# Grouped attention and convolution in one block of a two-block network: order of exponential and copy, of maxima, of keys' factors, of v's products and of the convolution's steps

## What is computed

```python
# even layer, h = rms_norm(x, norm_even): 512 x 1024
a_x, a_b, a_c, a_z, b_u, b_z = split(h @ w_in)            # six parts of 512 columns
conv = sum(pad(a_c * a_x)[:, tap:tap + s] * conv_w[tap] for tap in range(3))
y_a = a_b * conv * silu(a_z)
y_b = real(fft2(b_u)) * silu(b_z)
x = x + concatenate([y_a, y_b]) @ w_out
# odd layer, h = rms_norm(x, norm_odd): 8 heads of queries, 2 of keys and values, width 128
q, k, v, z = split(h @ w_in)
q, k = apply_rope(rms_norm(q, q_gain)), apply_rope(rms_norm(k, k_gain))
p = softmax(q @ k.T * 128 ** -0.5)                        # 512 x 512 for each of 8 heads
x = x + (concatenate(p @ v) * silu(z)) @ w_out
out = rms_norm(x, final_norm)
```

## Time and profile before

| what | us |
|---|---|
| median of 3 runs | 2379.01 |
| the profiled execution itself | 2379.91 |
| its span in the profile | 2378.1 |
| PE busy | 2148.1 (90%) |
| DVE busy | 1263.6 (53%) |
| POOL busy | 1059.9 (45%) |
| ACT busy | 825.9 (35%) |

### The profile page before, as it was taken

The page is one execution under the profiler, slowest core; times in us unless marked ns, Lnnn a source line. Parts: engine busy times, 40 slices in busy tenths (PEclk is TensorE's granted clock), DMA queues, the critical chain, the costliest instruction groups (busy, mean ns, idle before and its releaser), DMA issues.

```text
span 2378.1 us, 57690 instructions
## 1 busy us (share of the span) xinstructions
PE 2148.1 (90%) x23340; PEld 1810.4 (76%) x23340; DVE 1263.6 (53%) x1988; ACT 825.9 (35%) x2166; POOL 1059.9 (45%) x651
## 2 busy tenths in 40 slices
PE   6799999988999999985979989999897989898877
PEld 4598889978888888885979947777696866676555
DVE  6756566564665666666257414454315292457454
ACT  1644444444655555553021123333202001111431
POOL 1133343323333233327857802222585877775135
PEclk8899999999999999996989999999898999998999
DMA  2234433455344334413212211101022321221002
GB/s 92 90 128 157 151 147 147 168 161 113 69 90 92 72 68 92 92 43 119 95 58 85 89 45 36 35 18 36 27 88 97 109 73 43 66 93 54 18 1 71
DMA packets 158977, 197.86 MB, mean 83 GB/s; under 512 B 121040, under 2 KB 123344, under 8 KB 156496
## 3 DMA queue, kind: packets, MB, share of 16 engines
q1 hardware_dynamic: 158800, 195.25, 27.3%
HBM read 156.24 MB, written 38.99 MB: 82 GB/s over the span
## 4 chain that ended last, share of the span: by engine, by line
PE 54%; issue 7%; DVE 7%; POOL 5%; ACT 3%; POOLq 1%; DVEq 0%; ACTq 0%
PE wide L833 9%; PE wide L1310 8%; PE wide L1311 8%; PE wide L1312 8%; PE wide L1855 5%; PE wide L1964 2%; PE wide L1743 2%; PE wide L1920 1%; PE wide L1948 1%; PE wide L2220 1%; POOL x_w L1124 1%; ACT odd_probs L2540 1%; PE wide L858 1%; DVE odd_probs L2562 1%; POOL n_levels L1118 1%
## 5 line engine op out<-in xcount | busy, mean ns | idle before, releaser
L1310 PE MATMUL wide<-mixed_high,w_high_rwkv_in 128*128 128x264 f32 x720 | 211.1, 293 | 16.4 <-issue 9.3
L1312 PE MATMUL wide<-mixed_high,w_low_rwkv_in 128*128 128x264 f32 x720 | 206.6, 287 | 0.0
L1124 POOL TENSOR_TENSOR x_w<-n,masks 128x192 f32<-128x192 f32 x48 | 28.7, 598 | 361.3 <-ACT n L1001 361.3
L564 POOL TENSOR_TENSOR w_low_rwkv_in<-weights,w_high_rwkv_in 128x1024 fp32r<-128x1024 f32 x45 | 107.4, 2404 | 175.2 <-ACT w_high_rwkv_in L439 175.2
L355 PE MATMUL wide<-mixed_in,weights 128*128 128x264 f32 x672 | 160.6, 397 | 12.3 <-DVE mixed_in L325 12.0
L1331 POOL TENSOR_TENSOR w_high<-weights,con 128x1024 fp32r<-128x1024 f32 x52 | 125.8, 2419 | 99.3 <-PE wide L1312 59.8
L355 PEld LDWEIGHTS wide<-mixed_in,weights 128*128 128x128 f32 x672 | 127.6, 193 | 44.9 <-issue 16.2
L1310 PEld LDWEIGHTS wide<-mixed_high,w_high_rwkv_in 128*128 128x128 f32 x720 | 138.0, 192 | 29.2 <-issue 27.2
L1334 POOL TENSOR_TENSOR w_low<-weights,w_high 128x1024 fp32r<-128x1024 f32 x52 | 136.2, 2619 | 4.1
L1312 PEld LDWEIGHTS wide<-mixed_high,w_low_rwkv_in 128*128 128x128 f32 x720 | 137.9, 192 | 0.0
L833 PE MATMUL wide<-x_w,n_levels 64*64 64x64 f32 x2752 | 120.6, 223 | 4.2 <-DVE b_and_k L1061 0.3
(11 more groups left out here) (385 smaller groups left out, 6547.7 us busy)
## 6 DMA issues: line engine op xcount, KB each, us to landing
weights<-in_stream SPq DMA_DIRECT2D x200, 512.0 KB, 3.6
forms<-form SPq DMA_DIRECT2D x16, 2020.5 KB, 6.3
forms_in<-forms SPq DMA_DIRECT2D x96, 144.0 KB, 4.4
forms_in<-forms SPq DMA_DIRECT2D x32, 288.0 KB, 4.4
gate_bonus<-forms SPq DMA_DIRECT2D x16, 576.0 KB, 4.1
r_ahat_r<-forms SPq DMA_DIRECT2D x32, 144.0 KB, 3.6
mixed<-gate_bonus SPq DMA_DIRECT2D x14, 264.0 KB, 2.1
gated<-mixed SPq DMA_DIRECT2D x14, 264.0 KB, 4.7
```

What stands on the lines that cost most here:

```text
L564: pool.tensor_tensor(w_in[1][:, at, :], ring.slot(load), w_in[0][:, at, :].bitcast(F32), ALU.subtract).then_inc(w_split, 1)
L1310: pe.matmul(dst, w[0], x[0], start=start, stop=False)
L1312: return pe.matmul(dst, w[1], x[0], start=False, stop=stop)
```

## The change

Five places are edited. (1) In the even layer the first tap of the convolution moves from DVE to ACT (`act.activation(conv[:, t, :], ..., ACT.Identity, scale=...)`), counted by a new semaphore `tap`; the products `a_c * a_x` are made one with each A_X tile, the other two taps for one channel tile with each A_B tile, the product with `a_b` for one channel tile with each A_Z tile, and the gated output of channel tile t with Z tile t + 2. (2) In the odd layer the reciprocal and product of a key's factor are done by DVE two heads later, at heads i = 4 and 5 in place of 2 and 3. (3) The products for v are done by halves: first the four blocks with load ODD_V, in the order of the banks (`V_ORDER` = 2, 3, 0, 1), each waiting for its own bank; then the four blocks with load ODD_V + 1, whose split goes to a buffer of its own, `w_v` (over `odd_probs` and `odd_probs_t`), and waits for no tile. The counts of products and of loads are the same. (4) In the attention ACT issues the exponential of unit U + 1 ahead of the copy of unit U. (5) DVE makes the maxima two units ahead and after the product of the unit, in place of one unit ahead and before it.

```diff
--- before.py
+++ after.py
@@ -2163,7 +2163,7 @@
         conv = parts[:, A_X:A_X + 4, :]
-        g = {n: sem("g_" + n) for n in ("tanh", "tanh_made", "steps", "padded", "part_mm", "part_copied", "dft_mm", "y")}
+        g = {n: sem("g_" + n) for n in ("tanh", "tanh_made", "steps", "padded", "part_mm", "part_copied", "dft_mm", "y", "tap")}
 
@@ -2227,6 +2227,10 @@
             base = st.left
+            act.wait_ge(g["padded"], 2)
+            for t in range(4):
+                act.wait_ge(g["steps"], t + 1)
+                act.activation(conv[:, t, :], padded[:, t, 0:SEQ], ACT.Identity, scale=pcol("conv", t)).then_inc(g["tap"], 1)
             for n in range(24 - EVEN_FIRST):
@@ -2262,45 +2266,41 @@
 
-            def conv_step(tap):
+            def conv_step(t, tap):
                 after()
-                for t in range(4):
-                    w = pcol("conv", tap * 4 + t)
-                    src = padded[:, t, tap:tap + SEQ]
-                    if tap == 0:
-                        step(dve.tensor_scalar(conv[:, t, :], src, w, None, ALU.mult))
-                    else:
-                        step(dve.scalar_tensor_tensor(conv[:, t, :], src, w, conv[:, t, :], ALU.mult, ALU.add))
-            for n in range(A_X + 4):
+                step(dve.scalar_tensor_tensor(conv[:, t, :], padded[:, t, tap:tap + SEQ], pcol("conv", tap * 4 + t), conv[:, t, :], ALU.mult, ALU.add))
+
+            def conv_out(t):
+                tiles(A_B + t + 1)
+                after()
+                step(dve.tensor_tensor(parts[:, A_B + t, :], parts[:, A_B + t, :], conv[:, t, :], ALU.mult))
+
+            def gated(t):
+                after()
+                y = parts[:, A_B + t, :]
+                dve.scalar_tensor_tensor(y, y, 0.5, parts[:, A_Z + t, :], ALU.mult, ALU.mult).then_inc(g["y"], 1)
+            for n in range(A_X):
                 evict(n)
-            evict(A_B)
-            tiles(A_X + 4)
             for t in range(4):
+                evict(A_X + t)
+                tiles(A_X + t + 1)
                 step(dve.tensor_tensor(padded[:, t, 1:SEQ + 1], parts[:, A_C + t, :], parts[:, A_X + t, :], ALU.mult))
-            dve.wait_ge(g["padded"], 2)
-            for tap in range(3):
-                evict(A_B + 1 + tap)
-                conv_step(tap)
-
-            def conv_out():
-                after()
-                tiles(A_B + 4)
-                for t in range(4):
-                    step(dve.tensor_tensor(parts[:, A_B + t, :], parts[:, A_B + t, :], conv[:, t, :], ALU.mult))
-                after()
+            for t in range(4):
+                evict(A_B + t)
+                dve.wait_ge(g["tap"], t + 1)
+                conv_step(t, 1)
+                conv_step(t, 2)
             for n in range(8):
                 evict(EVEN_FIRST + n)
-                if n == 0:
-                    conv_out()
+                if n < 4:
+                    conv_out(n)
                 z = parts[:, A_Z + n, :]
...
                 dve.drain().then_inc(g["tanh"], 1)
-                if n < 4:
-                    after()
-                    y = parts[:, A_B + n, :]
-                    dve.scalar_tensor_tensor(y, y, 0.5, z, ALU.mult, ALU.mult).then_inc(g["y"], 1)
+                if 2 <= n < 6:
+                    gated(n - 2)
             st.left += 24 + SLOTS
@@ -2329,6 +2329,9 @@
         q_now = sh("q_now", 2, SEQ)
+        HH_V = ExitStack()
+        w_v = [HH_V.enter_context(nc.sbuf_tensor("w_v_" + n, [P, SLOT], mybir.dt.float32r))[:] for n in ("high", "low")]
+        HH_V.close()
         o_probs, o_probs_t = sh("odd_probs", 2, SEQ), sh("odd_probs_t", 2, SEQ)
@@ -2338,6 +2341,7 @@
         ODD_SCALE = P ** -0.5
+        V_ORDER = [(n + G_HEADS + G_KV) % SLOTS for n in range(4)]
 
@@ -2351,9 +2355,10 @@
         NORMED = [("q", 0), ("q", 1), ("k", 0), ("k", 1)] + [("q", n) for n in range(2, G_HEADS)]
+        K_LATER = 2
         STEPS = [0]
-        for kind, _ in NORMED:
-            STEPS.append(STEPS[-1] + (4 if kind == "q" else 6))
+        for i in range(len(NORMED)):
+            STEPS.append(STEPS[-1] + (6 if 0 <= i - G_KV - K_LATER < G_KV else 4))
         ALL_STEPS = STEPS[-1] + 3
@@ -2385,7 +2390,6 @@
         def dve_qk(dve, i, between):
-            kind, n = NORMED[i]
             x, y = with_gain[:, i % 2, :], head_of(i)
@@ -2398,11 +2402,13 @@
             dve.tensor_tensor(y, y, rot_sin[:], ALU.add).then_inc(o["dve"], 1)
-            if kind == "k":
+            n = i - G_KV - K_LATER
+            if 0 <= n < G_KV:
+                k = qk[:, G_HEADS + n, :]
                 dve.wait_ge(o["root"], n + 1)
...
                 after(5)
-                dve.tensor_tensor(y, y, qk_root[:, n, :], ALU.mult).then_inc(o["dve"], 1)
+                dve.tensor_tensor(k, k, qk_root[:, n, :], ALU.mult).then_inc(o["dve"], 1)
 
@@ -2421,16 +2427,19 @@
 
-            st.splits += 2
-            pe.wait_ge(w_split, st.splits)
-            w = [part[:].rearrange("p s (k n) -> p (s k) n", n=G_KV * P) for part in w_parts2]
-            for t in range(4):
-                pe.wait_ge(tile_left, st.left)
-                block = slice(t * P, (t + 1) * P)
-                for k in range(KD):
-                    mm = split_products(pe, wide[t][:, 0, 0:G_KV * P], [part[:, k, block] for part in u_odd],
-                                        (w[0][:, k, :], w[1][:, k, :]), k == 0, k == KD - 1)
-                mm.then_inc(o["v_mm"], 1)
+            for half, w in enumerate(([part[:, ODD_V % 2, :] for part in w_parts2], w_v)):
+                st.splits += 1
+                pe.wait_ge(w_split, st.splits)
+                for at, t in enumerate(V_ORDER):
+                    if half == 0:
+                        pe.wait_ge(tile_left, st.left - (3 - at))
+                    block = slice(t * P, (t + 1) * P)
+                    for k in range(KD // 2):
+                        mm = split_products(pe, wide[t][:, 0, 0:G_KV * P], [part[:, half * KD // 2 + k, block] for part in u_odd],
+                                            [part[:, k * G_KV * P:(k + 1) * G_KV * P] for part in w],
+                                            half + k == 0, half == 1 and k == KD // 2 - 1)
+                    if half == 1:
+                        mm.then_inc(o["v_mm"], 1)
             for k in range(2):
@@ -2456,8 +2465,8 @@
             st.left = base + SLOTS + 2 * G_HEADS + G_KV
-            for t in range(4):
-                act.wait_ge(o["v_mm"], t + 1)
+            for at, t in enumerate(V_ORDER):
+                act.wait_ge(o["v_mm"], at + 1)
                 act.activation(v_odd[:, t, :], wide[t][:, 0, 0:G_KV * P], ACT.Identity, scale=inv_column[:, t:t + 1]).then_inc(o["v_copied"], 1)
@@ -2532,13 +2541,19 @@
 
+        def act_exp(act, j, u):
+            U = UNITS * j + u
+            j, u = divmod(U, UNITS)
+            act.wait_ge(o["bias"], 2 * U + 2)
+            act.wait_ge(o["turned"], U + 1)
+            act.activation(o_probs[:, u % 2, :], S_BANK[u % 4], ACT.Exp, bias=o_bias[:, u:u + 1], scale=share_of(q_scale, j, u),
+                           accum_out=o_sum[:, u:u + 1]).then_inc(o["exp"], 1)
+
         def act_turn(act, j, last):
...
                 U = UNITS * j + u
-                act.wait_ge(o["bias"], 2 * U + 2)
-                act.wait_ge(o["turned"], U + 1)
-                act.activation(o_probs[:, u % 2, :], S_BANK[u % 4], ACT.Exp, bias=o_bias[:, u:u + 1], scale=share_of(q_scale, j, u),
-                               accum_out=o_sum[:, u:u + 1]).then_inc(o["exp"], 1)
+                if not (last and u + 1 == UNITS):
+                    act_exp(act, j, u + 1)
                 act.wait_ge(o["turned"], U + 3)
@@ -2554,12 +2569,12 @@
                 U = UNITS * j + u
-                if not (last and u + 1 == UNITS):
-                    dve_max(dve, j, u + 1)
                 dve.wait_ge(o["exp"], U + 1)
...
                 dve.tensor_scalar(o_probs[:, u % 2, :], o_probs[:, u % 2, :], o_sum[:, u:u + 1], None, ALU.mult).then_inc(o["share"], 1)
+                if not (last and u + 2 >= UNITS):
+                    dve_max(dve, j, u + 2)
                 if u in (4, UNITS - 1):
@@ -2610,6 +2625,7 @@
             act.drain().then_inc(o["pt"], 2)
+            act_exp(act, 0, 0)
             over_turns(act, act_turn, straight=True)
@@ -2617,6 +2633,7 @@
             dve_max(dve, 0, 0)
+            dve_max(dve, 0, 1)
             over_turns(dve, dve_turn, straight=True)
@@ -2624,7 +2641,13 @@
             pool_split_first(pool, FIRST["odd_in"], w_odd_first, w_parts2, (FIRST["odd_in"] - 2, FIRST["odd_in"] - 1))
-            pool_split(pool, (FIRST["odd_in"] + 4, 16), w_parts2)
+            pool_split(pool, (FIRST["odd_in"] + 4, 15), w_parts2)
+            ring.wait_full(pool, ODD_V + 1)
+            pool.tensor_tensor(w_v[0].rearrange("p (k n) -> p k n", k=KD), ring.slot(ODD_V + 1).rearrange("p (k n) -> p k n", k=KD),
```

(4 more changed lines are left out.)

## The result

| | median us | range | runs |
|---|---|---|---|
| before | 2379.24 | 2375.06 to 2380.3 | 4 |
| after | 2340.95 | 2337.38 to 2343.74 | 4 |

The ratio of the two is 0.9841 (95% interval 0.9824 to 0.9859): 38.3 us less. The profiled execution took 2341.08 us, span 2339.3.

A forecast was written before the change was run, and what follows sets the result against it. PE bounds where it is fed; targeted stalls were 7.6 + 5.5 + 23.0 us, plus slow clocks. Gains 20.9 + 9.2 - 2.5 + 5.4 = 33.0 us from 2379.9 give 2347 us, range 2338 to 2356.

The forecast's parts named there:

- Attention: Odd layer's attention: cutting the cycle through ACT and DVE shortens units from 2.82 to 2.40 us; gain 20.9 us.
- computed floor: Attention unit: PE's own work, 1.35 us from transposes to products with v plus 0.98 us for these, makes 2.33 us.
- The border: Between two attention turns: maximum and bias move ahead of the gate, so transposes to next transposes take 4.25 us.
- The last turn: Attention's final turn, without a border: 19.3 us plus 0.7 for POOL's splits of two loads, against 26.0 before; gain 6.0.
- Convolution: Even layer: less DVE work ahead of evictions removes 7.6 us of PE waits and 2.2 of slow clock; gain 9.2 us.
- The 0.6 us taken off: Even layer: deduction because DVE's operations meet POOL's splits on four tiles more and delay parts PE wants.
- Keys' factors: Odd layer: moved to heads 4 and 5, stalls of 2.2 and 5.3 us with slow clock replace one; loss of 2.5.
- rival (a): Odd layer: DVE operations fall between splits and the keys' stall goes, a gain of 6.9, total 2337.6 us; chance 0.13.
- v by halves: Odd layer: 6.1 us of idle or slow clock ahead of v go, 0.7 back at head 9; gain 5.4 us.
- (b): Even layer's end: DVE becomes the bound, 6.3 of the 9.2 us are given back, total 2353 us; chance 0.12.
- (c): Attention: something in DVE's line keeps units at 2.82 us, only borders gain 2.5 us, total 2365.4 us; chance 0.06.
- (d): Attention: each copy waits for a late exponential, 31 units cost 30 us more, total 2398 us; chance 0.04.

The follow-up runs named there:

- experiment 8: The changed kernel run again as it is: 2343.55 us, ratio 0.9847 to the kernel before; its table also compares eight profiles.
- experiment 1: Changed kernel with ACT's old order (exponential of U behind the copy of U - 1), maxima still two ahead: 2366.31 us, ratio 0.9932.
- experiment 3: Changed kernel with three of four blocks of keys in the product of probabilities and v, computation incomplete: 2329.44 us in one run.
- experiment 7: Changed kernel with the even layer's convolution in its old order, no tap on ACT: 2354.61 us, ratio 0.989.
- experiments 5 and 6: Changed kernel with keys' factors back at heads 2 and 3 (2336.93 and 2338.43 us), and changed kernel with v in one piece again (2346.66 us).
- experiment 5: Changed kernel with the keys' factors back at heads 2 and 3, measured twice: 2336.93 us and 2338.43 us.
- experiment 9: Changed kernel with the keys' reciprocals and products behind the last gate of their stage: 2332.12 us, ratio 0.9795.
- experiment 11: Changed kernel with keys' factors behind the stage's last gate and each turn's last gate behind the next turn's first product: 2328.78 us, ratio 0.9785.
- experiment 4: Changed kernel with the gate of unit 7 behind the first product and maximum of the next turn: 2335.55 us, ratio 0.981.

## Why the prediction was right, and where it was off

The forecast of 2347 us was 6 us above the median, and its sum of 33.0 us stands against 36.5 in the stages that the change touches (9.3 + 2.4 + 24.9 - 0.1), plus 2.3 us of scatter ahead of them. The closeness is in part that of one profile: in the other course of B to C (experiment 8) the stages behind A give 42.8 us.

**Attention: 20.9 forecast, 24.9 measured.** The mechanism is the one named: experiment 1 puts the cycle through ACT and DVE back and the 2.8 us with it, and experiment 3 shows PE's work as the limit after the change. Two terms were mis-sized. The unit was taken as 2.40 us and is 2.28, below even the computed floor of 2.33: 28 units by 0.12 are 3.4 us. The floor was a sum of two pieces from two different units of the old trace, 1.35 us from the transposes to the products with v, and 0.98; now the first piece is 2201.99 - 2200.70 = 1.29. In the old trace the transposes came after an idle time and took 0.65 us with their weight loads inside that; now the weights are loaded from 2200.59 on, under the last products with v, and they take 0.60. The border was taken as 4.25 us and is 3.90, three of them 1.0 us: the product took 0.49 us and not the 0.81 that was kept. It began at 2217.67, 0.11 us ahead of POOL's split. Of the two prices weighed in the prediction, the one by the Trainium skill (SBUF — State Buffer, "Who interferes with whom") was the better: the one that issues first keeps the port. The 0.9 us that it promised are most of these 1.0. The last turn took 0.6 us more than computed: from 2258.22 to the last gate at 2278.0 it is 19.8 us against 7 x 2.28 + 2.5 = 18.5, so 1.3 more where 0.7 was given; the longer units, one of 2.86 us and three of 2.5, stand beside POOL's four splits (2260.71 to 2270.55). The three, 3.4 + 1.0 - 0.6, are 3.8 of the 4.0 us.

**Convolution: 9.2 forecast, 9.3 measured.** No wait for an eviction is left, PE is busy for 72 of 72 us at full clock, and experiment 7 brings back 7.6 us of waits and a clock of 0.90. The moved products took 2.33 us at most, where 2.89 was feared, and the last four gates of z 1.52 or less, each after a wait of 0.7 us for its tanh; the last eviction started 116.2 us behind mark A, where it was 122.6. The 0.6 us taken off was not lost. ACT's Identity took 0.72 us (0.6 taken, up to 0.8 allowed), and nobody waited for it.

**Keys' factors: loss of 2.5 forecast.** Three stalls came, 2.2 us at head 5, 4.9 at head 6 (5.3 forecast) and 0.5 at head 9, and the move costs 2.4 or 2.9 us in the square of experiments 5 and 6. The first is as worked out. That the second came so near is luck: the gain product met the split (2.56 us, 0.5 in the sum) and the key's product did not (0.69, 1.4 in the sum), and PE wanted the product 9.0 us after the rotation before and not 7.3, as its tile ran in part at the lower clock. The prediction had the lower clock only as a cost behind a stall, and not as what decides the next one. So what it took for one course is more than one: its rival (a), in which operations fall between the splits, is half true in three of the eight profiles of experiment 8's table, where the stall at head 6 is missing. The move then costs nothing, and the stretch is 2.4 us shorter than with the factors at their own heads. Over the seven profiles of the table with v by halves B to C is 87.1 us on the mean, against 86.4 in the two profiles of experiment 5, so the cost of the move is under 1 us on this mean, and not resolved.

**v by halves: 5.4 forecast,** 4.8 or 5.3 measured by the same square, with 0.5 us of it given back at head 9.

**The rivals.** (b) and (c) are out by the rows of the even layer and by the unit of 2.28 us. Nothing of (d) is seen: the exponential of the next unit ended at 2200.33 with its row sum and the copy came at 2201.33, after 1.00 us in which ACT waited for PE's transposes. All 32 copies of the attention have such a wait for PE ahead of them, so no copy waited for an exponential.

## What to carry to other kernels

When two engines hand work to each other in a cycle, look for one instruction that can be issued one period early; here moving one exponential past one copy was worth 22.9 of the 38 us, with the same instructions. A step that is moved to where nobody waits for its result until much later is the better place for it, even if a first saving is already had elsewhere: the keys' factors lost time at either pair of heads, and putting them behind all heads gave 9 us against the first profile of the changed kernel and 4 against the second. Where operations of two engines hold one another up, as DVE's and POOL's did here, a shift of 1.2 us between them decided over a stall of 4.9, so look at more than one profile before a part is given a price.

## What was not expected of the hardware

The same wait was followed by different clocks. Ahead of the first transposes PE waited 2.18 us in experiment 9 and 2.19 in experiment 11, at the same point of the program. In the first the granted clock of the next 5 us is 1.00, in the second 0.66, and its first two units took 3.48 and 2.70 us in place of 2.42 and 2.28, which is 1.5 of the 1.6 us by which D to E is longer there than in experiment 4:

```profile
2189.00:2194.00 5.00, 4.46 (x26) 3.08 (x27) 3.78 (x10) 3.25 (x8) 0.61 (x1) 1.00 0.00 0
```

```profile
2185.00:2190.00 5.00, 4.47 (x19) 3.68 (x20) 3.22 (x9) 1.88 (x5) 0.61 (x1) 0.66 0.00 0
```

The wait of 2.23 us at head 5 is another such place: over the 6.5 us from the rotation that ended it the clock was between 0.55 and 1.00 in eight profiles (experiment 8). What decides between them wasn't tried and stays open. And a stall can be spared by lateness: in experiment 8 the split that would have held up two operations of DVE came 1.2 us later against DVE because PE's tile ran longer at the lower clock, and the execution was 4.3 us shorter for it.
